# Attention heads in the block of their projections; mLSTM convolutions summed in PSUM and copied out; two heads' value sums on ScalarE

## What is computed

```python
def forgetting_attention(h, k, v, F, w_qg, q_gain, w_o):
    qg = h @ w_qg
    q, gate = qg[..., :D_MODEL], qg[..., D_MODEL:]
    q = rms_norm(split_heads(q), q_gain).transpose(0, 2, 1, 3)
    # per block of 128 queries and each of 16 heads of 64:
    s = q @ k^T * 64 ** -0.5 + F_t - F_s     # masked to s <= t
    p = softmax(s);  o = p @ v
    return (o * jax.nn.sigmoid(gate)) @ w_o

def mlstm_inputs(...):                        # 256 context + 512 latent tokens
    xm, o_pre, z = jnp.split(hmod @ w_in, 3, axis=-1)
    xconv = depthwise 3 x 3 convolution of xm on a grid of 64 columns (context: one row)
    xconv = jax.nn.silu(xconv + conv_b)
    q = xh @ w_q;  k = (xh @ w_k) * DH ** -0.5       # 4 heads of 512, from xconv
    v = xm                                           # the same heads, not convolved
    gates = q @ wq_g + k @ wk_g + v @ wv_g
```

## Time and profile before

| what | value |
|---|---|
| median of three executions | 2944.92 us (2941.73 to 2947.05) |
| profiled execution, its own time | 2942.41 us |
| its span, first to last instruction | 2940.6 us |
| TensorE busy | 2763.0 us (94%) |
| GpSimd busy | 1487.2 us (51%) |
| VectorE busy | 1347.9 us (46%) |
| ScalarE busy | 766.4 us (26%) |
| granted TensorE clock, mean | 0.96 |

### The profile page before, as it was taken

One profiled execution on the slowest core, in us unless ns is written; L12 is line 12 of the kernel. 1 busy time (PEld: TensorE's weight loads), 2 busy tenths in 40 slices (PEclk: granted clock), 3 DMA queues, 4 the chain that ended last, 5 costly groups with the idle time before them and its releaser, 6 DMA issues. The chain is left out here.

```text
span 2940.6 us, 37066 instructions
## 1 busy us (share of the span) xinstructions
PE 2763.0 (94%) x15280; PEld 2164.9 (74%) x15280; DVE 1347.9 (46%) x1776; ACT 766.4 (26%) x1392; POOL 1487.2 (51%) x474
## 2 busy tenths in 40 slices
PE   5899788999999999989999998999999999999998
PEld 5777677788888765578888886767666457878887
DVE  6746356765512223327545287436076755020111
ACT  4553221411202224423111222222223423011210
POOL 3764615777767650057777442422263027754574
PEclk9999879999999999999999899999999999999999
DMA  5221317566522220025655212222242226221221
GB/s 235 84 75 59 81 47 286 209 226 235 214 86 86 86 72 1 1 102 213 226 203 187 99 62 86 90 79 90 90 168 101 95 102 251 106 90 58 72 97 60
DMA packets 84047, 353.64 MB, mean 120 GB/s; under 512 B 26680, under 2 KB 38968, under 8 KB 45888
## 3 DMA queue, kind: packets, MB, share of 16 engines
q1 hardware_dynamic: 66048, 243.05, 22.6%
q10 hardware_dynamic: 17856, 108.54, 10.0%
HBM read 316.94 MB, written 34.60 MB: 120 GB/s over the span
## 5 line engine op out<-in xcount | busy, mean ns | idle before, releaser
L484 POOL TENSOR_TENSOR whi<-wraw,con_sb 128x2048 fp32r<-128x2048 f32 x170 | 616.0, 3623 | 1351.2 <-PE ps L540 1136.3
L486 POOL TENSOR_TENSOR wlo<-wraw,whi 128x2048 fp32r<-128x2048 f32 x170 | 803.9, 4729 | 13.3
L540 PE MATMUL ps<-hh,whi 128*128 128x512 f32 x952 | 373.1, 392 | 5.0 <-DVE hl L1756 5.0
L540 PE MATMUL ps<-hl,whi 128*128 128x512 f32 x952 | 371.2, 390 | 0.0
L540 PE MATMUL ps<-hh,wlo 128*128 128x512 f32 x952 | 371.1, 390 | 0.0
L540 PEld LDWEIGHTS ps<-hh,whi 128*128 128x128 f32 x952 | 179.1, 188 | 45.8 <-DVE hl L1756 5.4
L1959 DVE TENSOR_TENSOR midl<-rsq,midh 128x512 fp32r<-128x512 f32 x64 | 154.8, 2424 | 113.8 <-ACT midh L1921 113.8
L540 PEld LDWEIGHTS ps<-hh,wlo 128*128 128x128 f32 x952 | 179.1, 188 | 37.5
L540 PEld LDWEIGHTS ps<-hl,whi 128*128 128x128 f32 x952 | 179.0, 188 | 37.0
L540 PE MATMUL ps<-midh,whi 128*128 128x512 f32 x512 | 200.4, 391 | 0.0
L540 PE MATMUL ps<-midh,wlo 128*128 128x512 f32 x512 | 200.0, 391 | 0.0
(11 more groups left out here) (411 smaller groups left out, 5303.3 us busy)
## 6 DMA issues: line engine op xcount, KB each, us to landing
wraw<-wst SPq DMA_DIRECT2D x174, 1024.0 KB, 4.8
cond_w<-wcond ACTq DMA_DIRECT2D x68, 1024.0 KB, 4.8
first_w<-wcond SPq DMA_DIRECT2D x8, 1024.0 KB, 19.7
mod_w<-wcond SPq DMA_DIRECT2D x8, 1024.0 KB, 14.3
d_v<-ssb ACTq DMA_DIRECT2D x4, 1536.0 KB, 5.5
d_s<-ssb ACTq DMA_DIRECT2D x4, 1536.0 KB, 5.5
sld<-d_s SPq DMA_DIRECT2D x4, 1536.0 KB, 8.2
vld<-d_v SPq DMA_DIRECT2D x16, 384.0 KB, 3.3
```

The source lines that it names most:

```text
L484: pool.tensor_tensor(whi[:, s], wraw[:, f], C("zero").broadcast_to([P, BLK]), ALU.add).then_inc(sem("w_high"), 1)
L486: pool.tensor_tensor(wlo[:, s], wraw[:, f], whi[:, s].bitcast(F32), ALU.subtract).then_inc(w_split, 1)
L540: o = e.matmul(ps[:, b, :nt], w[:, k, mc], x[:, k0 + k, t0:t0 + nt], start=first and k == 0 and j == 0, stop=final and k == nk - 1 and j == 2)
```

## The change

**Attention.** The two blocks become one. The heads' code stands behind the projections' code on each engine, with no meeting of the engines between them. New waits take the meeting's place: the first three scores and the first transposes wait for the gate tiles of the same banks to be read (`g_read`), and so does the first `gate`. `scale(0)` moves ahead of the last projection block, where it waits for the last of `pair_rows` and both low parts (`rows_made.at(3)`). VectorE's `norm` of the first pair then stands right behind `low_of`. `lengths` becomes two tiles at other places in SBUF, since its old place is used by the heads.

**Convolutions.** `conv` sums in PSUM banks 6 and 7 (`conv_acc`) rather than in the SBUF tile; the input and the weights stay in SBUF. An eleventh dependent step, a `tensor_copy`, brings the sum into the SBUF tile. There is one accumulator, and VectorE works in order. 

**Value sums.** For heads 0 and 3 VectorE's `value_sums` is left out. ScalarE reads each value tile twice: a Copy with scale -1 and an accumulator for the sum, then, after a wait for it, the Identity as before. For heads 1 and 2 nothing changes.

```diff
-        phase_start()
-        with nc.Block() as block:
-            norm_pe, norm_act, norm_dve, normed = norm_of_x(...)
...
+        lengths = [tiles(f"lengths{j}", at, shape=[16, T]) for j, at in enumerate((25, 69))]
...
                     if n >= 3:
                         pe.wait_ge(*raised.at(n - 2))
+                    else:
+                        pe.wait_ge(*g_read.at(n + 5))
...
                 def turn(n):
                     t = n % 4
+                    if n == 0:
+                        pe.wait_ge(*g_read.at(KT))
...
-                scale(0)
+                q0 = firsts["fq"][1]
+                block_by_tile(pe, q0, hh, hl, normed, bank_free=bank_free)
+                for j in range(1, 8):
+                    block_of(pe, q0 + j, 0, hh, hl, KT, 256, bank_free=bank_free)
+                    if j <= 4:
+                        length_sums(2 * j - 2)
+                        length_sums(2 * j - 1)
+                    if j == 6:
+                        pe.wait_ge(*rows_made.at(3))
+                        scale(0)
                 scores(0)
                 scores(1)
...
                 def gate(i):
+                    if i == 0:
+                        dve.wait_ge(*g_read.at(KT))
                     dve.wait_ge(*totalled.at(2 * i + 2))
...
                         act.wait_ge(*AC.need(acc_ready))
-                        act.wait_ge(*v_summed.at(6 * h + s + 1))
+                        if h in (0, HM - 1):
+                            act.activation(ssb[:, s], ps[:, b], ACT.Copy, scale=-1.0,
+                                           accum_out=vsum[:, s:s + 1]).then_inc(*v_summed.inc())
+                        v_count[0] += 1
+                        act.wait_ge(*v_summed.at(v_count[0]))
                         act.activation(ssb[:, s], ps[:, b], ACT.Identity, bias=vsum[:, s:s + 1],
                                        scale=512.0).then_inc(*AC.up(acc_taken))
...
+                conv_acc = ps[:, 6:8].rearrange("p b t -> p (b t)")[:, :TA]
+
                 def conv(h, m):
...
-                    y, z = xcs[r], xms[h % 2][:, m]
+                    if 4 * h + m:
+                        dve.wait_ge(sem("conv_done"), book.base.get(sem("conv_done"), 0) + 4 * h + m)
+                    y, z = conv_acc, xms[h % 2][:, m]
...
+                    dve.wait_ge(*VE.last())
+                    dve.tensor_copy(xcs[r], y).then_inc(*VE.up(sem("conv_done")))
...
-                    value_sums(h)
+                    if h in (1, 2):
+                        value_sums(h)
```

More of the change, by code:

```diff
@@ L2070, in program @@
         LOW = slice(32, 48)
+        otile = tiles("otile", 25, shape=[P, T])
+        pr, ptr = tiles("pr", 64, 4), [tiles(f"ptr{b}", 8 + 4 * b, 4) for b in range(2)]
+        oh, ol = tiles("oh", 48, KT, F32R), tiles("ol", 32, KT, F32R)
+        sums = fixed("sums", [P, 4, 2, 4])
+        top = fixed("top", [P, 4])
+        NI = 8 * KT
         phase_start()
@@ L2272, in _, with read_q, square_q, read_g @@
             def _(act):
+                def read_q(k):
+                    act.wait_ge(*AC.need(acc_ready))
+                    act.activation(q_sb[:, k], ps[:, k % NACC], ACT.Copy).then_inc(*q_read.inc())
+                def square_q(k):
+                    act.wait_ge(*q_read.at(k + 1))
+                    if k >= 2:
+                        act.wait_ge(*summed[0].at(k - 1))
+                    act.activation(qk_sq[:, k % 2], q_sb[:, k], ACT.Square).then_inc(*squared[0].inc())
+                def read_g(k):
+                    act.wait_ge(*AC.need(acc_ready))
+                    act.activation(g_sb[:, k], ps[:, k % NACC], ACT.Sigmoid).then_inc(*g_read.inc())
+                def root_of(j):
+                    act.wait_ge(*summed[j].at(KT))
+                    act.activation(lengths[j][:], ps[:16, 5 + j], ACT.Sqrt, bias=C("epsn")[:16],
+                                   scale=1.0 / 64).then_inc(*rooted.inc())
+                def high_of(j):
+                    act.wait_ge(*inverted.at(j + 1))
+                    act.activation(rms_split[:16, j], lengths[j][:], ACT.Copy).then_inc(*root_high.inc())
                 def exp(n):
```

164 lines of the change are left out of this document (64 added, 100 removed).

## The result

The changed kernel takes 2928.22 us, the median of five executions (2925.96 to 2930.81); the kernel before, run beside it, takes 2944.02 (2941.07 to 2947.05). The ratio is 0.9947, with an interval of 0.9933 to 0.9962: 11 to 20 us faster. The profiled execution takes 2928.82 us with a span of 2927.0, 13.6 less than before. The forecast was 2931.0, with a range of 2926 to 2941.

The account below looks back on a forecast made before the run. TensorE, busy 94% of the span, was taken as the bound, so edits pay only where it waits or runs at its lower clock. 2942.4 less 12.0 us (2.4 + 9.0 + 2.3 - 1.7) is 2930.4, forecast 2931, range 2926 to 2941.

Parts of the forecast that it names:

- The joint: Between projections and heads: without the meeting and the wait for norm, the first score starts 2.4 us earlier.
- the three covers: At the joint: scale(0)'s low part (1.3 us margin), the exponential's table load (0.5), and norm and g_read waits come in time.
- The clock: Behind the joint: if TensorE doesn't stop, the clock stays up; 9.0 us gained, 9.5 at most.
- The rival that the clock falls all the same: First attention pair: clock falls despite no stop, so only the gap is won, 2939.4 us; chance 0.18.
- The convolutions: mLSTM: taps 6.9 us beside GpSimd splits, a convolution 9.0; head 0's fourth ends 2.2 us earlier.
- the held low part: Head 0: low(0, 1), with two SBUF operands, is held by GpSimd until 1760.6 and ends at 1761.3.
- ScalarE's pair: Value tiles of heads 0 and 3: Copy, accumulator read and Identity take 1.35 us a tile, where it was 0.63.
- Head 0: mLSTM: first q tile starts 2.3 us earlier, range 0.3 to 4.3 depending on the clock.
- The last head: mLSTM: start hangs on the transfer, so ScalarE's pairs delay the first q tile 1.8 us; 1.7 lost taken.
- net 0.6 for the mLSTM: Head 0's 2.3 us gain less the last head's 1.7 us loss.
- The sum: Whole kernel: 2.4 + 9.0 + 2.3 - 1.7 = 12.0 us gained.
- The other rivals: Convolution taps still wait for GpSimd (2935.2 us, chance 0.05), or chained PSUM taps are dear (2964 at 1.6 us, 0.05).

Follow-up runs that it names:

- e5: Changed kernel, with TensorE held before the first score by three idle VectorE multiplications after the last gate's read (2.86 us pause); 2943.19 us, ratio 1.0002.
- e7: Kernel before, meeting kept, with seven idle TensorE products between scale(0) and the first score; 2933.86 us, ratio 0.9969.
- e1: Changed kernel's merged attention block alone, with the mLSTM inputs of the kernel before; 2932.03 us, ratio 0.9969.
- e3: Changed kernel, but ScalarE sums the values of head 0 only, VectorE those of heads 1 to 3; 2929.04 us, ratio 0.9956.
- e4: Changed kernel, but all value sums on VectorE, so only the PSUM convolutions remain of the mLSTM edits; 2926.86 us, ratio 0.9956.
- e9: Changed kernel with all value sums on VectorE and head 0's conv(0, 3) ahead of low(0, 1); 2925.51 us, ratio 0.9944.
- e12: Changed kernel itself run again, unaltered, as yardstick for the three runs beside it; 2930.78 us, ratio 0.9963.
- e8: Changed kernel, but scale(0) behind the last projection block as before, so only the meeting is gone; 2935.66 us, ratio 0.998.
- e6: Changed kernel with one TensorE wait for the last gate's read before the first score (0.69 us pause); median 2930.99 us of four, profiled execution 2938.14.
- e2: Changed kernel's mLSTM inputs alone (PSUM convolutions, ScalarE sums in heads 0 and 3), attention in two blocks as before; 2940.19 us, ratio 0.9989.
- e11: Changed kernel, all value sums on VectorE, conv(0, 3) ahead of low(0, 1), plus 8 and 18 idle TensorE products in heads 0 and 3; 2921.82 us.
- e10: Changed kernel, all value sums on VectorE, plus 10 and 18 idle TensorE products in the value waits of heads 0 and 3; 2921.67 us.

## Why the prediction was right

**The joint, 2.4: right.** From the gate's read to the first score it was 2.86 us and is -0.11, 2.97 less; the pair ahead takes 0.45, net 2.5. The pause is 0.1 and not 0. None of the three covers gave way: TensorE shows no wait ahead of `scale(0)`, and the exponential at 1094.04 (forecast 1093.7) was in time for the transpose at 1094.98 (forecast 1094.8).

**The clock, 9.0 of at most 9.5: right in mechanism, and 9.4 in size.** First to ninth score took 22.83 us (1094.22 to 1117.05) and takes 13.42 (1092.02 to 1105.44), and behind that the two kernels agree: 125.77 us to the last exponential in both. Fourth to ninth takes 10.26, where the forecast had 10.3. The 0.4 between 9.0 and 9.4 was kept back for waits without `values` between the scores, and they didn't come. That the *cause* is TensorE's pause was an argument in the prediction; e5 and e7 show it. The rival that the clock falls all the same, with a chance of 0.18, is out at the pause of 0.1 us: all eight traces with that joint (after, e1, e3, e4, e9 to e12) have an attention leg of 139.03 to 139.08. But the margin was small, as e8 and e6 show with falls behind 1.27 and, once, 0.69 us.

**The convolutions: right.** Taps 6.90 (forecast 6.9), first step 1.02 and copy 0.96 (1.0 each), whole convolution 9.1 with what lies between (9.0). An estimate by the Trainium skill, "VectorE: DVE Perf Modes", section "The TRN2 errata", made ten taps 0.65 us longer with a PSUM source. They are 0.04 longer (6.90 for 6.86), so the page's difference isn't seen, as the prediction chose by the earlier trace rows. From the first xm read, the held low part ends at 44.4 us (forecast 44.5: 1761.3 less 1716.76, the read in the kernel before by the table's first three legs) and the fourth convolution at 53.4 where it was 55.7: 2.3 us earlier, forecast 2.2. So of the 15 us that faster taps free in head 0, some 2 count, as the sum had it.

**ScalarE's pair, 1.35: 1.28 to 1.30. Head 0, 2.3: 3.2.** The first q product starts 2.5 us earlier after the first xm read. The further 0.7 is the clock: in the 10 us from that product it is 0.90, which is 2.0 us at the lower level, and was 0.82, or 3.6 us; the difference of 1.6 costs 0.8. The prediction left that out of the sum as unknown, plus or minus 2. e4 shows that ScalarE's sums, to which the prediction tied this gain, aren't what does it: VectorE's sums of 0.6 us each keep up as well once the fourth convolution is early.

**The last head, 1.7 lost: 2.1.** From the first value tile's start on ScalarE to the first q product it is 4.14 us (2059.19 to 2063.33) and was 2.34: 1.8 later, as forecast. Behind that the clock decides. Against e4 the head loses 2.4, of which the pairs are 0.9 (after less e3) and the longer fall the rest, and the loss isn't seen at the end of the span. So the sum's net 0.6 for the mLSTM is 1.1 by the two legs, and 0.6 to 5.9 by the timed runs of e2 (its interval, of 2942).

**The sum.** 2.5 + 9.4 + 3.2 - 2.1 = 13.0 where 12.0 was forecast, and the unchanged legs add 0.6 to it in the profiled execution. The ratios make 15.6 us for the first set of runs and 10.9 for the second (e12), and the intervals of both hold 13. The other rivals are out: no tap waits for GpSimd, and none in the dependent chain is above 0.75 us (line 2641, 160 taps, at most 748 ns).

## What to carry to other kernels

Look for a short pause of TensorE with light work behind it, and price it by the clock of the next 20 us, not by its length: here 2.9 us of pause cost 12.4, and seven idle products bought back 9.2 of it. Taking out a barrier alone isn't enough if a wait of a microsecond is left behind it; move the work that feeds the first instruction ahead of the last full block. Where VectorE is held up by GpSimd, keeping the running sum in PSUM ended it here, but count the gain only to the next instruction that still has both in SBUF and to the next wait of the engine that takes the result.

## What the runs showed of the hardware

- The granted clock fell behind pauses of 2.90 (0.94 and 1.26, with 0.7 of products between), 2.86, 1.27 and once 0.69 us at the joint, and stayed low for 17 to 24 us of scores and transposes. It stayed at 2.4 GHz behind 0.1 us (eight traces), and behind 0.94 us followed by 2.2 us of products (e7).
- In front of dense weight products the same kinds of pause cost less: in the mLSTM's first head a fall lasts 3.6 us behind 3.51, 0.64 and 0.28 us, and none comes behind 1.75 us (e11), while one comes behind 2.50 (e10). The length isn't fixed by the wait: in the last head, in the same code, the fall lasts 6.8 us behind 4.72 in e3 and 3.6 behind 4.73 in e4.
- No step of the sixteen convolutions that has PSUM as operand or output was held beside GpSimd's splits: first steps of 1.01 to 1.02 us, taps of 6.89 to 6.90, copies of 0.96. Without PSUM, a subtraction of two SBUF tiles of 0.96 us took 3.69, and a multiplication of one by a column, SBUF to SBUF, 3.67 to 3.76 for 0.62.
- ScalarE's read of the accumulator is 0.19 to 0.20 us, and makes Copy and Identity of 128 x 512 a pair of 1.29 us.
- A longer last head went with a shorter rest: 85.6 with 828.8, 83.3 with 831.8, in nine of the kernels, though the rest is unchanged code. (e5 and e6 don't fit, with 86.5 and 830.2, 85.8 and 831.7.) Only filling TensorE's wait there shortened both (82.26, with 825.7 and 824.8).
